# When VectorE adds the identity in the two-lane RWKV stage: behind the mask of the keys' reads instead of ahead of it

## The reference, cut to what matters

```python
def step(S, xs):
    r, w, k, v, a, b = xs
    sa = jnp.einsum('bhvk,bhk->bhv', S, a)
    S = S * w[:, :, None, :] + sa[..., None] * b[:, :, None, :] + v[..., None] * k[:, :, None, :]
    return S, jnp.einsum('bhvk,bhk->bhv', S, r)
```

## Time and profile before

| | us |
|---|---|
| median of the three runs | 3863.41 |
| the profiled execution's own time | 3858.04 |
| its span, first to last instruction | 3856.2 |
| TensorE busy in the span | 3547.2 (92%) |
| VectorE busy | 2038.4 (53%) |
| ScalarE busy | 1541.8 (40%) |
| GpSimd busy | 250.7 (6%) |
| mean granted TensorE clock | 0.965 of full |

### The profile page before, as it was taken

One profiled execution on the slowest core, in us unless ns is written; L12 is line 12 of the kernel. 1 busy time (PEld: TensorE's weight loads), 2 busy tenths in 40 slices (PEclk: granted clock), 3 DMA queues, 4 the chain that ended last, 5 costly groups with the idle time before them and its releaser, 6 DMA issues. The chain is left out here.

```text
span 3856.2 us, 71009 instructions
## 1 busy us (share of the span) xinstructions
PE 3547.2 (92%) x31292; PEld 2932.6 (76%) x31292; DVE 2038.4 (53%) x3564; ACT 1541.8 (40%) x2599; POOL 250.7 (6%) x295
## 2 busy tenths in 40 slices
PE   6788989999898998989999799989999999999998
PEld 3566666766666676768888789847989799999877
DVE  1454454544455447774665556655444555555444
ACT  2333343333333333454544444425443444444433
POOL 0001111011111112002000000010000000000000
PEclk9899999999999999999999799999999999999999
DMA  9423323242333416443325354414553555555554
GB/s 379 144 70 97 112 86 117 70 128 84 117 101 97 128 44 234 151 138 113 109 91 185 128 164 136 154 61 155 184 181 125 175 175 175 182 180 185 190 182 163
DMA packets 349473, 548.57 MB, mean 142 GB/s; under 512 B 11724, under 2 KB 119916, under 8 KB 346988
## 3 DMA queue, kind: packets, MB, share of 16 engines
q1 hardware_dynamic: 346716, 538.78, 42.9%
q10 hardware_dynamic: 2448, 5.24, 0.4%
HBM read 535.86 MB, written 8.13 MB: 141 GB/s over the span
## 5 line engine op out<-in xcount | busy, mean ns | idle before, releaser
L302 PE MATMUL lane<-r,r 128*128 128x256 f32 (+1 forms) x8520 | 1506.9, 326 | 50.4 <-DVE r L260 40.4
L260 DVE TENSOR_TENSOR r<-ring,r 128x1024 fp32r<-128x1024 f32 x770 | 941.2, 1229 | 944.9 <-ACT r L299 943.6
L302 PEld LDWEIGHTS lane<-r,r 128*128 128x128 f32 x8520 | 1279.5, 193 | 207.7 <-DVE r L260 45.7
L302 PE MATMUL bank<-r,r 128*128 128x512 f32 (+2 forms) x6360 | 1402.2, 359 | 36.3 <-DVE r L260 24.8
L302 PEld LDWEIGHTS bank<-r,r 128*128 128x128 f32 x6360 | 1055.0, 195 | 241.9 <-issue 52.2
L299 ACT ACTIVATE r<-ring 128x1024 fp32r<-128x1024 f32 x770 | 808.8, 1056 | 957.1 <-PE lane L302 570.9
L302 PE MATMUL lane<-arena 64*64 64x64 f32 (+4 forms) x12940 | 622.6, 254 | 68.3 <-DVE arena L260 23.9
L302 PEld LDWEIGHTS lane<-arena 64*64 64x64 f32 (+3 forms) x12940 | 468.7, 140 | 234.2 <-issue 111.1
L299 ACT ACTIVATE arena<-lane 128x256 f32<-128x256 f32 (+3 forms) x578 | 248.8, 451 | 558.5 <-PE lane L302 446.4
L260 DVE TENSOR_TENSOR arena<-arena 128x256 f32<-128x256 f32 (+7 forms) x568 | 255.6, 481 | 35.8 <-ACT arena L299 14.9
L271 DVE COPY arena<-lane 128x256 f32<-128x256 f32 (+3 forms) x366 | 131.8, 362 | 267.2 <-PE lane L302 249.6
(11 more groups left out here) (94 smaller groups left out, 1252.2 us busy)
## 6 DMA issues: line engine op xcount, KB each, us to landing
ring<-in_w_gate_up SPq DMA_DIRECT2D x88, 1024.0 KB, 5.0
ring<-in_mod_w SPq DMA_DIRECT2D x73, 1024.0 KB, 5.2
ring<-in_ev_w_in SPq DMA_DIRECT2D x44, 1024.0 KB, 8.4
ring<-in_w_down SPq DMA_DIRECT2D x44, 1024.0 KB, 5.0
ring<-in_od_w_in SPq DMA_DIRECT2D x40, 1024.0 KB, 5.1
ring<-in_w_in SPq DMA_DIRECT2D x40, 1024.0 KB, 5.1
ring<-in_w_xkv SPq DMA_DIRECT2D x32, 1024.0 KB, 5.3
ring<-in_ev_w_out SPq DMA_DIRECT2D x28, 1024.0 KB, 5.2
```

What stands on the lines that cost most here:

```text
L260: return Nothing() if self.e is None else self.e.tensor_tensor(o, a, b, op)
L302: return Nothing() if self.e is None else self.e.matmul(o, l, r, start=start, stop=stop)
```

## The change

The three additions and the wait ahead of them leave the VectorE part of `P_LR` and stand behind the mask in that of `KR`, when h is 1. Operands, buffers and semaphores are the same. `own()` now waits for the mask of KR1 where it waited for the mask of L and R.

```diff
     def P_LR(d, n, bp):
...
              M.SI[d].unsqueeze(1).unsqueeze(1).to_broadcast([P, 2, 2, P]), MUL) \
             .then_inc(*v.n(("free", *bp[0]), ("free", *bp[1]), ("LR", d, n, 0)))
-        own()
-        v.tt(s.Z[1][:, 0, :, 1, :], s.LR[:, :, 0, 0, :], M.C("i64").unsqueeze(1).to_broadcast([P, 2, 64]), ADD) \
-            .then_inc(*v.n(("TT1", d, n)))
-        for q in range(2):
-            at_, to = slice(64 * q, 64 * q + 64), slice(64 - 64 * q, 128 - 64 * q)
-            v.tt(s.Z[1][to, 1, :, 1, :], s.LR[at_, :, 1, 0, :], M.C("i64")[at_, :].unsqueeze(1).to_broadcast([64, 2, 64]), ADD) \
-                .then_inc(*v.n(("TT1_1", d, n)))
 
     def KR(d, n, h, b):
         s = M.lane[d]
...
             full(b)
             v.tt(s.KR.rearrange("p h c a n -> p (h c) (a n)"), c4(M.bank[b[0]]),
                  M.SI[d].unsqueeze(1).to_broadcast([P, 4, P]), MUL).then_inc(*v.n(("free", *b), ("KR", d, n)))
+            own()
+            v.tt(s.Z[1][:, 0, :, 1, :], s.LR[:, :, 0, 0, :], M.C("i64").unsqueeze(1).to_broadcast([P, 2, 64]), ADD) \
+                .then_inc(*v.n(("TT1", d, n)))
+            for q in range(2):
+                at_, to = slice(64 * q, 64 * q + 64), slice(64 - 64 * q, 128 - 64 * q)
+                v.tt(s.Z[1][to, 1, :, 1, :], s.LR[at_, :, 1, 0, :], M.C("i64")[at_, :].unsqueeze(1).to_broadcast([64, 2, 64]), ADD) \
+                    .then_inc(*v.n(("TT1_1", d, n)))
```

## The result

The changed kernel took 3858.3 us, median of 20 runs (3849.58 to 3863.91); the kernel before, over 20 runs beside them, 3864.8 (3859.18 to 3874.33). The ratio is 0.9979, with a 95% interval of 0.9972 to 0.9986: 8.1 us faster (5.4 to 10.8), about 0.2%. The ratio is estimated from all the runs and is not the quotient of the two medians, which lie 6.5 us apart. Forecast were 3852.6, that is 10.8 us, and a range of 3847 to 3864. The direction and the mechanism of the order held. The gain was less, and much of what follows is about which part of the sum was too large.

A forecast was written before the change was run, and what follows sets the result against it. VectorE's backlog was taken to bound the 6 us around the change in each pair. Order -6.3 and clock -4.5 gave -10.8 us, from 3863.4 to a forecast of 3852.6 us, range 3847 to 3864.

The forecast's parts named there:

- The bound: In the 6 us around the change, in each of 16 pairs, VectorE's backlog is the bottleneck and TensorE waits for it.
- The slot: One triple of additions on VectorE costs 1.05 us; five long waits give 1.0 to 1.1 each, 5.2 us in all.
- The overlap: A copy behind additions was taken to start 0.04 us after their end; by the skill's rule, 0.1 earlier, sum 0.5 lower.
- The short waits: Six pairs where TensorE has fill: the gain is the short wait itself, 1.8 us in all.
- The pairs with a split: Five pairs with an ev_split ahead of double0(0)'s copy: three lose 0, one 0.1, the third 0.6; together +0.7 us.
- The clock: TensorE's low-clock stretches behind three long waits, in the sixth, eighth and tenth pair, all go: 3 x 1.5 = -4.5 us.
- The order's -6.3: Gain from VectorE's new order alone, over all 16 pairs: -5.2 - 1.8 + 0.7 = -6.3 us.
- The first rival: The order pays, the clock does not, as low-clock stretches move elsewhere: 3857.1 us; chance 0.27.
- Rival 2: Gain swallowed: the projection's weight loads land at their old times and TensorE waits longer; 3863 to 3861 us; chance 0.17.
- Rival 3: Slower: additions right ahead of double0(0)'s copy hurt wherever VectorE is not late; 3873 us if all pairs do; chance 0.10.
- The point of 1.9 us: The change turns to a loss when KR products end later than 1.9 us after lane 0's additions used to start.

The follow-up runs named there:

- e6_busy_kr: Kernel before, with TensorE making the products of KR1(1) six times instead of once in the sixth, eighth and tenth pair: 3858.86 us, ratio 0.9987.
- e1_lane1_only: Kernel before, with only lane 1's additions moved behind the mask of KR1, lane 0's left in place: 3853.64 us, ratio 0.9971.
- e5_double: Kernel before, in its old order, with lane 1's additions and their wait made twice in a row: 3879.67 us, ratio 1.0038.
- e2_lane0_only: Kernel before, with only lane 0's additions moved behind the mask of KR1, lane 1's left in place: 3862.28 us, ratio 0.9999.

## Why the prediction was right, and where its size was off

**The bound.** Right. VectorE's backlog, not TensorE's products, set this place, and lane 1's additions stood in it. (In one detail the reading was off: VectorE did not come straight from `keys` in the twelfth pair, an `ev_split` of 1.22 us stood between, which lengthens the backlog.) The two half-changes show it from both sides: 11.2 us for lane 1's alone, nothing for lane 0's alone; and the doubled triple costs 0.96 in D0 in ten pairs alike.

**The slot.** The prediction had the copy of double0(0) 1.05 earlier in the twelfth pair and the third doubling 1.0 earlier at most. Measured were 1.21 in D0 and 1.05 in D2. The copy gained 0.1 more because it isn't held (see "The overlap"), and the rest because the masks now follow each other without a break; little of that reached D2. So the close agreement of D2 with 1.05 is in part luck. In the doubled kernel a further triple costs 0.96, since it follows additions and not a mask.

**The short waits.** Forecast 1.8 us over six pairs. Measured in D2 in the three profiles: second pair 0.71, fourth 0.75, 0.14 and 0.54, fifth 0.03, eleventh 0.57, thirteenth a loss of 0.79 once and a gain of 0.26 and 0.25 twice, sixteenth 0.37. The sums are 1.6, 2.1 and 2.5 us: right in size. In the one loss VectorE waited 1.13 and 0.42 us for TensorE's products, as it does in the third pair.

**The pairs with a split.** The third lost 0.61, 0.61 and 0.60 against the first profile of the kernel before, where 0.6 was forecast, and 0.7 against the mean of all three. The ninth, for which I had written 0, lost 0.8 to 1.2 against the first profile, but one of the other profiles before has 0.8 too, so only part of it is the change's. In it, the load of the projection's weights was issued 2.5 to 2.8 us ahead of the first mask, and 3.6 in the first two profiles before; in the third of before, the one with the same loss, it was 2.6. It can be a small piece of the second rival.

**The clock.** This is the term that was mis-sized: "I take it that all three low stretches go: 3 x 1.5 = -4.5 us". At the eighth and tenth pair it held: the low clock had cost 1.5 us there (at the eighth, D2 was 9.97 in the kernel before and 8.46 in `e6_busy_kr`, which has the same order), and in the changed kernel the cost is gone in all three profiles. The sixth pair's stretch was chance, there in one profile of three. And over the whole program the clock did not rise: by the mean granted clocks of the runs the term is 0.6 us, give or take 1.5, not 4.5. The order's -6.3 alone is near what was measured, 8.1 (5.4 to 10.8) by the ratio and 6.5 by the medians. The first rival, with 3857.1, was the better forecast of the time (3858.3 measured); the range was wide enough to hold both. The Trainium skill's page "TensorE: Matmul & The Clock Gate", Part 1, says that the clock's switching varies from run to run of the same kernel; the profiles agree (the low time in the stage was 75.1 to 88.7 us in three of the kernel before), and I had given too little weight to it.

**The overlap.** The rule of "VectorE: DVE Perf Modes", section "Two Vector instructions with no wait between them", in the Trainium skill, held, and my own row did not carry over. The copy starts at 1077.10, 0.07 before the additions end at 1077.17; the mask behind the copy starts at 1077.54, 0.03 after the copy's end, where before it overlapped by 0.08. The rule's 0.1 us a pair is there at the first copy and is paid back at the next mask.

**The rivals.** Rival 2 (swallowed): ScalarE's waits for the projection's weights were 101.8 to 104.5 us in the three profiles before and 102.1 to 104.0 in the three after, and the pairs' starts moved to earlier times step by step in `e1_lane1_only`, by 9.1 us at the sixteenth. So these loads did not land at their old times. In the changed kernel half of what the pairs gained was given back between them, above all at a block of the modulation; the two other kernels make it unlikely that this is the rival at work, but no run shows its cause. Rival 3 (slower): its mechanism is real. It has its price in the third pair each time, where the KR products came late, and it came up in the thirteenth pair in one profile of three (0.79 us). The point of 1.9 us was not tested between.

**What stays open.** Over the whole program the clock gave the change little or nothing. What is not shown is why: whether the stretches that went at two pairs bring on others, or whether others fall as they do in any run. `e6_busy_kr` took away the same idling, and the clock of its runs rose; its one profile doesn't show where.

## What to carry to other kernels

Where an engine with low average use is named at the end of a wait, look at what stands ahead of the awaited instruction in its queue, and who needs that: work which nobody needs yet belongs behind. Moving more than that gained nothing that could be shown: the triple that stood in an idle gap (lane 0's) cost 0.6 us in the third pair when it was moved, and the kernel that left it alone had the lower median (3853.64 against 3855.48). Don't count low-clock stretches one by one from a single profile: some are there in one profile and not in the next. Compare the mean granted clock over all runs of both kernels.

## What the runs showed of the hardware

- In the twelfth and fourteenth pair TensorE waited 1.44 and 1.34 us and kept the full clock in all three profiles of the kernel before; with waits of 2.39 and 2.30 in `e5_double` it fell to the low clock. In the eighth pair the low clock came with waits of 2.56 and 2.57, and with 1.48 in `e1_lane1_only` and `e2_lane0_only`; with 0.38 and 0.39 it didn't. Such a stretch costs these dependent small products 1.5 us. More work on TensorE, in place of idling, made the kernel faster by 5.0 us (1.5 to 8.5), with a mean granted clock of 0.9663 against 0.9637.
- GpSimd's additions of 128x128 took 0.41 us each, where VectorE's took 0.29, and those of 64x128 0.42 against 0.29. VectorE's copies and masks kept their mean lengths in that kernel (422 and 684 ns).
- A VectorE copy out of PSUM started 0.07 us before the end of an addition that worked on half the partitions; a mask with a constant from SBUF, behind the same kind of addition, started 0.04 us after its end.
